# Two transformer-like blocks on one core: the hand-overs between five stages, and three steps inside the attentions' pairs, at other places in the order

## The reference, cut to what matters

```python
def per_layer_embedding(h, p_i, norm_g, w_gate, w_proj):
    return h + (p_i @ w_proj) * jax.nn.sigmoid(rmsnorm_2(h, norm_g) @ w_gate)
# stick-breaking attention, for a block of 128 queries:
z = jnp.einsum('bhtd,bhsd->bhts', q, k)
log_keep = jnp.where(strict, jax.nn.log_sigmoid(-z), 0.0)
suffix = lax.cumsum(log_keep, axis=3, reverse=True) - log_keep
weights = jnp.where(strict, jnp.exp(jax.nn.log_sigmoid(z) + suffix), 0.0)
out = weights @ v          # then * silu(gate), then @ w_out
```

## Time and profile before

| | |
|---|---|
| median of 3 runs | 3135.73 us (3134.46 to 3139.21) |
| the profiled execution, its own time | 3134.45 us |
| its span, first to last instruction | 3133.0 us |
| granted TensorE clock, mean | 0.990 |
| TensorE matmuls, busy | 3042.1 us, 97% of the span |
| VectorE, ScalarE, GpSimd busy | 59%, 45%, 21% |

### The profile page before, as it was taken

How to read it: one execution, slowest core, us unless ns; L and a number is a source line. 1 busy time by engine, 2 the same in 40 slices (tenths; PEclk the granted TensorE clock), 3 DMA queues, 4 the chain that set the end, 5 groups by cost and what they waited for, 6 DMA issues and landing times. The chain is left out here.

```text
span 3133.0 us, 39543 instructions
## 1 busy us (share of the span) xinstructions
PE 3042.1 (97%) x15324; PEld 2541.0 (81%) x15324; DVE 1839.8 (59%) x2502; ACT 1396.3 (45%) x2104; POOL 660.6 (21%) x444
## 2 busy tenths in 40 slices
PE   8999999999999999999999999998999999998998
PEld 6888888888888878787887878877878888886787
DVE  4444223666666634367667576676557777777544
ACT  5333213555555423335244252443346666666531
POOL 0210002222223200302010020110235555544210
PEclk9999999999999999999999999998999999999999
DMA  3111222211112234112121121211121111112422
GB/s 111 52 47 49 67 74 68 74 55 61 55 55 67 81 120 147 53 36 81 41 74 54 41 81 48 74 48 61 34 101 41 41 41 41 39 42 75 155 99 76
DMA packets 58807, 208.44 MB, mean 67 GB/s; under 512 B 6928, under 2 KB 9872, under 8 KB 58512
## 3 DMA queue, kind: packets, MB, share of 16 engines
q1 hardware_dynamic: 49360, 174.16, 16.5%
q0 software_dynamic: 9280, 31.99, 3.3%
HBM read 170.87 MB, written 26.87 MB: 63 GB/s over the span
## 5 line engine op out<-in xcount | busy, mean ns | idle before, releaser
L119 ACT ACTIVATE whi<-wraw 128x1024 fp32r<-128x1024 f32 x208 | 218.4, 1050 | 418.5 <-PE a_D L132 64.2
L124 DVE TENSOR_TENSOR wlo<-wraw,whi 128x1024 fp32r<-128x1024 f32 x173 | 237.5, 1373 | 156.7 <-ACT whi L119 155.6
L130 PE MATMUL ssm_D<-x1hi,whi 128*128 128x512 f32 x640 | 257.5, 402 | 0.0
L130 PE MATMUL b_D<-x1hi,whi 128*128 128x512 f32 x640 | 254.1, 397 | 0.0
L132 PE MATMUL ssm_D<-x1hi,wlo 128*128 128x512 f32 x640 | 250.5, 391 | 0.0
L131 PE MATMUL ssm_D<-x1lo,whi 128*128 128x512 f32 x640 | 250.4, 391 | 0.0
L132 PE MATMUL b_D<-x1hi,wlo 128*128 128x512 f32 x640 | 250.2, 391 | 0.0
L131 PE MATMUL b_D<-x1lo,whi 128*128 128x512 f32 x640 | 249.9, 391 | 0.0
L2644 DVE TENSOR_TENSOR_SCAN stick_keep<-stick_keep,stick_first 128x896 f32<-128x896 f32 (+7 forms) x128 | 214.6, 1680 | 41.9 <-ACT stick_keep L2531 41.4
L2796 POOL TENSOR_TENSOR stick_rows<-stick_rows,stick_keep 128x896 f32<-128x896 f32 (+7 forms) x128 | 161.1, 1261 | 257.8 <-DVE stick_keep L2644 241.6
L130 PE MATMUL a_D<-x1hi,whi 128*128 128x512 f32 x512 | 201.8, 394 | 12.3 <-DVE x1lo L159 12.3
(11 more groups left out here) (458 smaller groups left out, 7680.3 us busy)
## 6 DMA issues: line engine op xcount, KB each, us to landing
wraw<-w_dram SPq DMA_DIRECT2D x208, 512.0 KB, 3.6
sq<-acum_rows SPq DMA_DIRECT2D x32, 512.0 KB, 3.8
att_bias<-alibi_dram SPq DMA_DIRECT2D x16, 512.0 KB, 3.8
stack<-stack POOLq DMA_DIRECT2D x32, 256.0 KB, 3.7
f<-y_b SPq DMA_DIRECT2D x11, 512.0 KB, 5.7
x_sb<-xT_dram SPq DMA_DIRECT2D x8, 512.0 KB, 8.8
branch_a<-sq POOLq DMA_DIRECT2D x8, 512.0 KB, 3.5
y_b<-att_y POOLq DMA_DIRECT2D x8, 512.0 KB, 3.0
```

Source lines behind the costliest of these rows:

```text
L119: act.activation(self.whi[:, s, :, :], self.wraw[:, s, :, :], ACT.Copy).then_inc(self.w_hi, 1)
L124: dve.tensor_tensor(self.wlo[:, s, :, :], self.wraw[:, s, :, :], self.whi[:, s, :, :].bitcast(F32), ALU.subtract).then_inc(self.w_lo, 1)
L130: pe.matmul(out, self.whi[:, s, w0, :], xhi[:, k, cols], start=start, stop=False)
```

## The change

No arithmetic is changed; one small activation per pair is new.

- **A, att's pairs:** on VectorE, `normalise(p, 15)` moves from the head of slot 16 behind that slot's `low_weights`.
- **B, att to pb:** the split of the projection's first weight tile moves ahead of the barrier, to the end of att; `dense_by_parts` is new and makes pb's first product of y: for each k it waits for the high part and issues the four matmuls that need only that, then waits for the low part and issues the last two.
- **C, ssm to ple0:** the last split leaves the end of ssm and stands behind the high parts (on VectorE the low parts) of ple0's input. `dense_by_parts` makes the first gate tile. `embed(0)` moves from ahead of the second gate tile to between `norm_sums` and `norm_spread`. The split for the third tile moves ahead of the root. VectorE makes the low part of p when its high part is there, not when both are.
- **D, ple0 to stick:** the four constants are written behind the scaling of the first half tile.
- **E, stick's pairs:** `head_sums` of the keys moves ahead of `turn_weights` in slot 6.
- **F, stick's pairs but the last:** a sigmoid of one column into a new tile `spare` stands ahead of `part_y(p, 7)`.
- **G, stick to sout:** the first four `output_parts` move into slots 11 to 14 of the last pair, and their low parts into slots 12 to 15.

```diff
@@ -141,6 +141,20 @@
+
+    def dense_by_parts(self, pe, out, s, xhi, xlo, hi_ready, lo_ready):
+
+        for k in range(KT):
+            pe.wait_ge(hi_ready, k + 1)
+            for half in range(2):
+                cols = slice(half * H, half * H + H)
+                pe.matmul(out[:, cols], self.whi[:, s, k, :], xhi[:, k, cols], start=k == 0, stop=False)
+                pe.matmul(out[:, cols], self.wlo[:, s, k, :], xhi[:, k, cols], start=False, stop=False)
+            pe.wait_ge(lo_ready, k + 1)
+            for half in range(2):
+                cols = slice(half * H, half * H + H)
+                last = pe.matmul(out[:, cols], self.whi[:, s, k, :], xlo[:, k, cols], start=False, stop=k == KT - 1)
+        return last
@@ -979,6 +993,7 @@
                 pair(p, p % 2, p < PAIRS - 1)
+            split(PAIRS + 1, 1)
@@ -1055,12 +1070,14 @@
                 for slot in range(19):
-                    if 1 <= slot <= 16:
+                    if 1 <= slot < 16:
                         normalise(p, slot - 1)
...
                         low_weights(p, unit, g)
+                    if slot == 16:
+                        normalise(p, 15)
                     if slot < 16:
@@ -1092,6 +1109,8 @@
                 pair(p, p % 2, p < PAIRS - 1)
+            dve.wait_ge(dn, 8 * (PAIRS + 1) + 1)
+            K.split_lo(dve, 2 * (PAIRS + 1) + n0 // 2, 1)
@@ -1143,7 +1162,10 @@
                     pe.wait_ge(prod, i)
-                K.dense(pe, D2[:, :], 1, yhi, ylo, y_lo if i == 0 else None).then_inc(mm, 1)
+                if i == 0:
+                    K.dense_by_parts(pe, D2[:, :], 1, yhi, ylo, y_hi, y_lo).then_inc(mm, 1)
+                else:
+                    K.dense(pe, D2[:, :], 1, yhi, ylo).then_inc(mm, 1)
@@ -1178,7 +1200,6 @@
-            K.split_hi(act, n0 // 2, 1)
             for k in range(KT):
@@ -1217,7 +1238,6 @@
             dve.sem_inc(m_done, 1)
-            K.split_lo(dve, n0 // 2, 1)
             for k in range(KT):
@@ -1737,7 +1757,7 @@
                                bias=K.eps[:, 0:1]).then_inc(root_done, 1)
-                for m in range(4):
+                for m in range(4 if g < GROUPS - 1 else 3):
                     split(g, 12 + m, 24 + 4 * m)
@@ -1969,7 +1989,7 @@
                         dve.tensor_tensor(f_sb[:, j, cols], f_sb[:, j, cols], tmp[:, cols], ALU.add).then_inc(scaled, 1)
-                    if j % 2 == 1:
+                    if j % 2 == 1 and not (g == GROUPS - 1 and j == KT - 1):
                         split(g, 12 + j // 2)
@@ -2003,6 +2023,7 @@
+PARTS_SLOT = 11
 EMBED_HALVES = {4: (0,), 5: (1,), 6: (2,), 7: (3,), 8: (4,), 9: (5,), 10: (6,), 11: (7,), 12: (8,), 13: (9,),
@@ -2098,16 +2119,18 @@
                     pe.wait_ge(scaled, j - 1)
-                if j < KT - 1:
-                    K.dense(pe, D[:, s, :], s, xhi, xlo, x_lo if j == 0 else None).then_inc(mm, 1)
                 if j == 0:
-                    pe.wait_ge(p_lows, 2)
+                    K.dense_by_parts(pe, D[:, s, :], s, xhi, xlo, x_hi, x_lo).then_inc(mm, 1)
+                elif j < KT - 1:
+                    K.dense(pe, D[:, s, :], s, xhi, xlo).then_inc(mm, 1)
                 if j == 1:
...
                     K.norm_sums(pe, sums, sums_done)
+                    pe.wait_ge(p_lows, 2)
+                    embed(0)
                     K.norm_spread(pe, spread, rtok_done, 1, spread_done)
                     pe.wait_ge(r_done, 1)
-                if j < KT - 1:
+                if 0 < j < KT - 1:
                     embed(j)
@@ -2118,15 +2141,18 @@
                 K.tile_hi(act, xhi, f_sb, k, name, x_hi)
+            K.split_hi(act, n0 // 2, 1)
             act.wait_ge(landed, 32)
...
                 K.square(act, f_sb[:, k, :], k, sq_done, acc_done)
+            act.wait_ge(mm, 1)
+            K.split_hi(act, n0 // 2 + 1, 0)
             K.norm_root(act, sums, DM, sums_done, root_done)
...
                 sigmoid(act, n)
-                if n < KT - 2:
+                if 0 < n < KT - 2:
                     act.wait_ge(mm, n + 1)
@@ -2140,16 +2166,19 @@
                 K.tile_lo(dve, xlo, xhi, f_sb, k, name, x_hi, x_lo)
+            K.split_lo(dve, n0 // 2, 1)
+            dve.wait_ge(parts, 1)
+            dve.tensor_tensor(p_lo[:, :, :], p_raw[:, :, :], p_hi[:, :, :].bitcast(F32), ALU.subtract).then_inc(p_lows, 1)
             dve.wait_ge(parts, 2)
-            dve.tensor_tensor(p_lo[:, :, :], p_raw[:, :, :], p_hi[:, :, :].bitcast(F32), ALU.subtract).then_inc(p_lows, 1)
             dve.tensor_tensor(w_lo[:, :, :, :], w_raw[:, :, :, :], w_hi[:, :, :, :].bitcast(F32),
...
             K.sum_squares(dve, KT, sq_done, acc_done)
+            K.split_lo(dve, n0 // 2 + 1, 0)
             K.norm_recip(dve, root_done, rtok_done)
...
                 scale(dve, n)
-                if n < KT - 2:
+                if 0 < n < KT - 2:
                     K.split_lo(dve, n // 2 + (n0 // 2 + 1), n % 2)
@@ -2197,6 +2226,7 @@
         gains = sb("gains", [P, 1])
+        spare = sb("spare", [P, PAIRS])
         select = sb("select", [P, 2])
@@ -2422,9 +2452,11 @@
                         values(p, q, unit, g)
+                    if more and slot == AUX_SLOT["k_sum"]:
+                        head_sums(p + 1, 0)
                     for unit, g in turns_of(slot):
                         turn_weights(p, unit, g)
-                    if more:
+                    if more and slot != AUX_SLOT["k_sum"]:
                         aux(p + 1, slot)
@@ -2587,13 +2619,15 @@
                             embed_copy(n)
+                        if PARTS_SLOT <= slot < PARTS_SLOT + KT // 2:
+                            output_parts(act, slot - PARTS_SLOT)
                     if more:
                         ahead(p + 1, 1 - q, slot)
-                if not more:
+                if more:
+                    act.activation(spare[:, p:p + 1], K.eps[:, 0:1], ACT.Sigmoid)
+                else:
                     for n in EMBED_HALVES[18]:
                         embed_copy(n)
-                    for k in range(KT // 2):
-                        output_parts(act, k)
                 part_y(p, 7)
@@ -2740,11 +2774,10 @@
                         ahead(p + 1, 1 - q, slot)
+                    elif PARTS_SLOT < slot <= PARTS_SLOT + KT // 2:
+                        output_low_parts(dve, slot - PARTS_SLOT - 1)
                 if more:
                     scale(p + 1, 1 - q, 3, 1)
-                else:
-                    for k in range(KT // 2):
-                        output_low_parts(dve, k)
                 add_y(p, 7)
@@ -2764,13 +2797,14 @@
             K.norm_copy(dve, scores, spread_done, r_done)
-            dve.wait_ge(landed, 16)
-            dve.memset(first[:, 0:S - P], 0.0).then_inc(masks, 1)
-            dve.tensor_copy(first[:, S - P:S], K.ident[:, :]).then_inc(masks, 1)
-            dve.memset(keep[:, :, S:S + 1], 0.0).then_inc(masks, 1)
-            dve.tensor_tensor(gains[:, :], K.gain("q_g", 0), K.gain("k_g", 0), ALU.mult).then_inc(masks, 1)
             for slot in range(19):
                 ahead(0, 0, slot)
+                if slot == half_done_slot(0, 0) + 1:
+                    dve.wait_ge(landed, 16)
+                    dve.memset(first[:, 0:S - P], 0.0).then_inc(masks, 1)
+                    dve.tensor_copy(first[:, S - P:S], K.ident[:, :]).then_inc(masks, 1)
+                    dve.memset(keep[:, :, S:S + 1], 0.0).then_inc(masks, 1)
+                    dve.tensor_tensor(gains[:, :], K.gain("q_g", 0), K.gain("k_g", 0), ALU.mult).then_inc(masks, 1)
             scale(0, 0, 3, 1)
...
                 pair(p, p % 2, p < PAIRS - 1)
```

## The result

The changed kernel takes 3119.34 us (median of 5 runs, 3113.11 to 3121.21); the kernel before took 3135.85 beside it. The ratio is 0.9941 (95% interval 0.993 to 0.9952): 16.5 us faster, where 15 were forecast. The profiled run spans 3116.8 us; the page's part 1 has 8.7 us less of matmul time than the earlier trace rows.

The account below looks back on a forecast made before the run. TensorE's matmuls fill 97% of the span; idle time costs its length plus slow matmuls behind it. Seven terms sum to -14.3 us from 3134.45, giving 3120.1 profiled, 3121 as median; range 3113 to 3130.

Parts of the forecast that it names:

- its bound of 2.7: At att to pb: the forecast's upper limit, +2.7 us, reached if the clock's fall costs 3 us.
- It gains at most 0.4 us: At pb's second tile: TensorE arrives at most 0.4 us earlier, since the weight's low part follows y's last landing.
- gave back 2 of 3 us: Behind the copy of R in ple0: shorter idle stretches recover 2 of about 3 us lost to the lower clock.
- the head sums late by 0.8 for `sq`: At stick's head: the keys' head sums would wait 0.8 us for ScalarE's square, leaving a gain of 0.2.
- I take 0.2 off each start: At six stick pairs' starts: the scan, started 0.8 us earlier, mostly waits for GpSimd; 0.2 gained each, -1.2 in all.
- that rule: VectorE operations with two SBUF inputs and GpSimd's exclude each other; the scan's end stays fixed, so the early sigmoid gains 0.
- the term for the crowded last pair: In the last stick pair: moved output parts find little idle time; 3.0 us, plus 0.6 for a clock fall.
- the hand-overs give nothing: Rival, chance 0.22: changes between stages don't pay, only the att scaling and stick head sums pay in full; 3128.
- The slower side: Rival, chance 0.04: the clock falls once in each of seven stick pairs and at three new idle times; 3144.

Follow-up runs that it names:

- two_rows: The kernel before with only two moves: att's last row scaled behind low_weights, stick's head sums ahead of turn_weights; 3127.2 us, ratio 0.9966.
- low_parts_moved: Changed kernel, last pair: sout weight's low part in slot 6, not 2; embedding operand's second low part ahead of row 4's scan; 3115.5 us, ratio 0.9926.
- all_mended: Changed kernel with pb's second weight made early, the keys' first square ahead of a weight split, and two last-pair low parts moved; 3105.3 us, ratio 0.9898.
- late_product2: all_mended with GpSimd's output product behind the next pair's first two rows (first seven pairs), second weight's low part one slot later; 3115.3 us, ratio 0.9931.
- no_f: Changed kernel without the spare sigmoid, so the table load is back at each pair's start; 3118.5 us, ratio 0.9938.
- no_g: Changed kernel with the first four output parts and their low parts back behind the last pair; 3120.0 us, ratio 0.9945.
- after: The changed kernel itself, with all parts of the change, against the kernel before; 3119.3 us, ratio 0.9941.
- no_b: Changed kernel with pb's entry as before: weight split behind the barrier, first product in the old order; 3119.3 us, ratio 0.9942.
- late_product: Changed kernel with GpSimd's output product of a stick pair behind the next pair's first two rows' products; 3125.7 us, ratio 0.9963.
- late_product3: late_product2 with GpSimd's gains at slots 3 and 4 and its gate at slot 5, behind rows 2 and 3; 3096.4 us, ratio 0.9867.

## Why the prediction was right

The total held (3119.3 against 3121), and the mechanisms of A, C and E came as written, F's but for its gain at each start. But the sum was right in part because errors cancelled: A and E gave 4.3 more than forecast, C and G 2.2, against 1.6 at B, 1.8 at D, 1.0 at F and 2.2 in the last pair ahead of G; another 1.6 is the fall in ple1 that did not come this time.

- A, right in mechanism, 4.6 for 6.5. The scaling ends 0.3 behind GpSimd, at 655.55, as forecast. The term was mis-sized since I multiplied the listed idle time and not the distance from start to start. With the 0.27 found here it is 7 x 0.93.
- B, +1.3 for +2.9, above its bound of 2.7 in that profile (its own terms give 2.6), and -0.5 to +3.1 over seven. The two waits (2.7 and 3.8, forecast 2.6 and 4.1) and the chain between them were as described. What failed is "It gains at most 0.4 us": I took y's landings as fixed to the tenth, and the last one moves by up to 1.8 us from one execution to the next.
- C, right in mechanism: -5.6 for -6.4 in this profile. ple_D's wait is 2.2 shorter (forecast 2.4), the new one 0.79 (0.9), and of the 7.0 us at the copy of R 3.5 are C's (3.6). The clock didn't fall behind it at all (27 matmuls in the 6.1 us from 2167.7 on, where the earlier trace rows has 14), where I gave back 2 of 3 us. How much of this is C's is not settled: of the twelve profiles with C nine have -4.15 behind ple_D's first product and three, with a fall of 3.4 us near the norm, -2.5; and two_rows, without C, had 3.4 instead of 6.8 us at 0.50 there, and gained 1.0. No run takes C out alone.
- D, wrong in sign: -0.2 for +1.6 (1.5 to 3.1 in seven profiles with D, 0 to 1.2 in three without). I saw the late square ("the head sums late by 0.8 for `sq`", measured 0.84) and priced it at its length. What failed is that I did not ask what a new wait ahead of 1.9 us of tiny matmuls does to the clock, though I had asked it for C and G.
- E, right in mechanism: -3.7 for -6.1, by the same start to start as A. Its 0.53 became 0.87. The other 0.65 in the balance is one pair of the kernel before, which was that much longer than its neighbours.
- F, -1.2 for -0.2 at most (6 x 0.04). What failed is "I take 0.2 off each start": the scan began 0.83 earlier and ended at the same place. The Trainium skill (SBUF — State Buffer, "Who interferes with whom") was the better forecaster: by that rule F was worth 0. The runs agree: 3.35 us beside GpSimd's product, 2.02 without it, and the scan ends 1.9 us behind GpSimd, with F and without; an operation that started earlier beside GpSimd's ended no earlier.
- G, -0.3 for about -1.7. Its gains are right (2.3 of wait and 1.6 by the clock; the other 1.6 us, a fall in ple1, came and went between profiles whatever G was). Its cost was 2.2, not 3.6: the term for the crowded last pair was mis-sized.
- Not in the sum at all: the long fall in the last pair. The pair has 17 to 24 us at 0.50, in one or two falls, in every changed kernel but low_parts_moved and all_mended, 13.6 before, and the stretch is up to 3.6 longer for it. That its length hangs on the pair's own waits is shown by low_parts_moved and by the wait of 1.9 at stick_pO, though late_product2 and 3, which have the same two steps moved, still ran 17 us at 0.50. Why that wait stands in some profiles and not in others with the same code there is open, and so is why the kernel before had less: E ends ahead of this pair, and two_rows, no_f and no_g have the long fall alike.

Of the rivals, "the hand-overs give nothing" holds for B and D alone, and C and G paid, by the profiles. The slower side didn't show: the pairs keep the full clock.

## What to carry to other kernels

Price a wait by the starts of the matmuls around it, not by the listed idle time; for half a microsecond of idle the difference is over 0.2 us, and it repeats in every pair. When a start is moved earlier, look at what it reaches next: in B, D and F the gain was lost to one operation that stood behind another engine's landing or port, and moving that operation (a weight loaded ahead of the barrier, a square ahead of a split, GpSimd's product behind the rows), with two low parts moved in the last pair, gave 23 us on top of the change's 16.5.

## What was new of the hardware

- The same code behind the same wait had the lower clock for 3.4 or 6.8 us, or not at all, from profile to profile: behind pb's second wait (2.4 to 3.8 us) 3.4 in five profiles, 6.8 in one and none in one; in stick's head 3.4 twice (after), or 6.8 once (no_b, no_g, no_f); in ple1 behind 0.6 us of wait in seven of fourteen kernels. A fall of 3.4 us cost about 1.7 (pb). By estimate from these, a hand-over read from one profile is good to about 2 us, and the whole kernel to 3 or 4.
- GpSimd and VectorE with two SBUF inputs: a scan took 2.02 alone and 3.35 beside a product that had begun 0.94 earlier; a low part of 1.20 took 2.27 or 2.64. The price depends on where the two meet: in late_product a scan of 256 columns, begun 1.0 behind a GpSimd operation of 2.39 with another right behind that, took 3.88 instead of 0.68. So GpSimd's operations should lie where VectorE has time to spare; late_product3 found such places.
- Of y's four tiles loaded behind the barrier, with four other loads of 512 KB beside them, the third was there 9.1 to 9.6 us behind att's last matmul and the fourth 11.2 to 13.0, with the same code.
